# A two-block transformer kernel in f32: GpSimd's weight sums and tap matrices rescheduled, and the first products of three stages reordered

## The chip, the cores and the metric

The kernel runs on one core of one Trainium2 chip. The metric is the device time of one execution in microseconds (us). In the profile PE is TensorE, DVE is VectorE, ACT is ScalarE, POOL is GpSimd and SP is SyncE, which issues most DMAs.

## The reference, cut to what matters

The reference is a stack of residual layers in f32 over 512 positions of width 1024 (the later layers also carry 256 context positions). In order: latent attention, a squared-ReLU MLP, a gated mixer (`sgu`), a second MLP, a final norm, then a second network: convolution, an rwkv mixer, attention, convolution and the output norm. The parts that matter here are these.

```python
h = rms_norm(x, norm_mix[i]);  x = x + mixer(h)                      # x @ w_o ends each mixer
h = rms_norm(x, norm_ffn[i]);  x = x + square(relu(h @ w_up)) @ w_down
# gated mixer: z = gelu(h @ w_in); u, v = split(z); ...; (u * v) @ w_out
# convolution: a, b, gate = split(h @ w_in, 3); y = a * sigmoid(b)
#              y = depthwise_conv(y, 31 taps); y = silu(layernorm(y)); (y * silu(gate)) @ w_out
```

## The kernel before, in words

The activations lie transposed in SBUF: `xs` is the residual and `hn` the normed input, each 128 partitions by 8 rows of blocks (k = 0 to 7) by 768 positions.

**Products with fewer multiplications.** Twelve weight matrices (list `BLOCKED`) go through `pair_products`. One chunk of weights gives two output blocks from seven block products instead of eight (the Winograd form of Strassen's scheme). Each of the seven is a call of `product`: four matmuls of 128x256. It takes either a raw weight block (A0, A1, A3) or a sum of blocks (S1 to S4), and either a quarter of the input (b11, b21, b22) or a sum of quarters (t1 to t4). b11 and b12 are rows k = 0 to 3 of the input, b21 and b22 are rows 4 to 7; t1 = b12 - b11, t2 = b22 - t1, t3 = b22 - b12, t4 = t2 - b21. `mla_out` has 4 chunks, `up0` and `up1` 16 each, `sgu_u` 8, `sgu_out` and `attn_out` 4 pairs of 2 chunks, `down0` and `down1` 4 pairs of 4.

**Who makes the operands.** POOL makes the weight sums in `weight_sums` (lines 3321 to 3344): four additions of 128x512 for each chunk n, in the order of the chunks. For n >= 2 it waits until PE has finished chunk n - 2 (`chunk_mm` at n - 1), which frees the place of the sums. DVE makes t1 to t4 in `block_sums` (line 2611), counted by the semaphore `t_ready`. PE takes the seven products in a fixed order: A0, A1, S2, S3, S1, A3, S4. For the first chunk of a stage (`early`) three quarters of S4 come right behind A1, since S4 needs no sum of the input.

**Who empties the banks.** Products land in four quarter banks. ACT copies the first (`take_p1`), and DVE adds the parts in `take_first`, `take_second` and `take_third` (lines 2627 to 2654). PE may write a quarter again once `bank_ev` has reached its count.

**Stage borders.** `mla_out` and `sgu_out` end in `block_residual` (line 2678). For each of four pairs p it adds two rows into `xs` (line 2689) and writes the scaled rows of `hn` for the next MLP (line 2695), and each written row raises `h_ready` by one. Rows come as 2p + 1 and 2p, so that rows 0 to 3 are there after p = 1. The MLP's first product waits for all eight (`up_need`, line 1146). Behind `down0` comes a norm: ACT squares, POOL adds most squares, PE sums over partitions, ACT takes the root, DVE the reciprocal (line 2438) and eight SCALAR_TENSOR_TENSOR (line 2446) that give `hn`; then come `block_sums` and the stage `sgu_u`.

**Attention's last round.** The loop of units U has 8 rounds of 8 units i. In each unit DVE takes a maximum (line 3286), negates it (3288), waits for ACT's exponential, takes a reciprocal (3302) and scales the probabilities (3304). In the last round two block sums for `attn_out` stand in unit 5 and two in unit 6.

**The second convolution.** `conv` (name `c1`) starts with a norm of the residual. POOL adds six of the eight blocks of squares in `partial_sum` (line 3346), PE then adds that sum and the last two blocks over the partitions in `norm_sums`, and ACT and DVE finish the norm. The convolution of one of the eight rows of channels (k = 7) is done on PE, with 31 diagonal matrices that POOL builds in `tap_matrices` (line 3365): 31 TENSOR_SCALAR of 128x128. POOL's program ends with these lines:

```python
            weight_sums("attn_out")
            tap_matrices(1, chunk_mm, Q["attn_out"].chunk1)
            partial_sum("c1", SEQ, hn)
            partial_sum("last", SEQ, hn)
```

An engine runs its own program in order; a wait holds all that stands behind it.

Of the kernel before, what the change touches and what calls it, by code (L numbers as in the profile page):

```python
# [247 lines left out]
def build(nc, t):  # L248
# [18 lines left out]
    with ExitStack() as ctx:  # L267
# [647 lines left out]
        def _(pe):  # L915
# [190 lines left out]
            def pair_products(name, p, c, B, need):  # L1106

                b, B = Q[name], B[c]
                g, n = b.pair0 + p, b.chunk(p, c)
                end, first = bank_mm if c == b.per - 1 else None, c == 0  # L1110
                halves_need = name == "mla_out" and p == 0
                lo, hi = slice(0, HALF), slice(HALF, SEQ)

                def take(b_):
                    if first and g:
                        pe.wait_ge(bank_ev, bank_free(g - 1) + b_ + 1 if g - 1 != PAIR0 + WIDE_PAIRS - 1 else bank_free(g))

                pe.wait_ge(raw_full[raw_turn(n)], raw_count(n))
                take(0)
                need(c, 0)  # L1120
                product(name, p, c, quad_ps[0][:, lo], first, True, "A0", B["b11"])
                if halves_need:
                    need(c, -1)
                product(name, p, c, quad_ps[0][:, hi], first, False, "A1", B["b21"], end)
                early = p == 0 and c == 0
                if early:
                    take(3)
                    product(name, p, c, quad_ps[3][:, lo], first, True, "S4", B["b22"], ks=range(3))
                take(1)
                need(c, 2)  # L1130
                product(name, p, c, quad_ps[1][:, lo], first, True, "S2", B["t2"])
                need(c, 3)
                product(name, p, c, quad_ps[1][:, hi], first, False, "S3", B["t3"], end)
                take(2)
                product(name, p, c, quad_ps[2][:, lo], first, True, "S1", B["t1"])
                need(c, 4)
                product(name, p, c, quad_ps[2][:, hi], first, False, "A3", B["t4"], end)
                if not early:
                    take(3)
                product(name, p, c, quad_ps[3][:, lo], first, True, "S4", B["b22"], chunk_mm, ks=range(3, 4) if early else range(4))  # L1140

            def ffn(i, nrm):

                up, down = Q[f"up{i}"], Q[f"down{i}"]

                def up_need(c, t):
                    if t:
                        pe.wait_ge(t_ready, T_BASE[f"up{i}"] + t)
                    else:
                        pe.wait_ge(h_ready, 8 * (NI[nrm] + 1))  # L1150

                def down_need(c, t):
                    if t:
                        pe.wait_ge(t_ready, T_BASE[f"down{i}"] + 4 * c + t)
                    else:
                        pe.wait_ge(hid_ready, HID_BASE[i] + 8 * (c + 1))

                for p in range(up.pairs):
                    pair_products(f"up{i}", p, 0, up_b, up_need)
                    if p == 3:  # L1160
                        norm_sums(nrm, SEQ, seq_only(fsq[i]))
                    if p in UP_MOD_SUMS:
                        q = UP_MOD_SUMS.index(p)
                        mod_sums(MOD_UP[i] + q, up_macc[q % 2])
                for p in range(down.pairs):
                    for c in range(down.per):
                        pair_products(f"down{i}", p, c, down_b, down_need)
# [7 lines left out]

            def sgu_u_need(c, t):

                if t:
                    pe.wait_ge(t_ready, T_BASE["sgu_u"] + t)
                else:  # L1180
                    pe.wait_ge(h_ready, 8 * (NI["sgu"] + 1))

            def sgu_out_need(c, t):

# [1244 lines left out]
        def _(dve):  # L2429
# [178 lines left out]
                        o(stt(a, w, c, a, ALU.mult, ALU.add), (sig["half"] if k == 3 else sig["macc"] if k == KD - 1 else None) if v else None)  # L2608
                    last_step[v] = o.last

            def block_sums(B, ahead=True, rest=True):

                b11, b12, b21, b22, t1, t2, t3, t4 = [B[n] for n in ("b11", "b12", "b21", "b22", "t1", "t2", "t3", "t4")]
                T = sig["t"]
                if ahead:
                    o(nc.vector.tensor_tensor(t1, b12, b11, ALU.subtract), T)
                    o.wait()
                    o(nc.vector.tensor_tensor(t2, b22, t1, ALU.subtract), T)
                    T.two = T.n
                if rest:  # L2620
                    o(nc.vector.tensor_tensor(t3, b22, b12, ALU.subtract), T)
                    dve.wait_ge(T.sem, T.two)
                    o(nc.vector.tensor_tensor(t4, t2, b21, ALU.subtract), T)

            add = nc.vector.tensor_tensor

# [70 lines left out]
            block_sums(mla_b[0])  # L2697
            for p in range(Q["mla_out"].pairs):
                block_residual("mla_out", p, gain=0)

            def ffn(i, nrm):
                up, down = Q[f"up{i}"], Q[f"down{i}"]
                dve.wait_ge(h_ready, 8 * (NI[nrm] + 1))
                block_sums(up_b[0])
                for p in range(up.pairs):
                    g = up.pair0 + p
                    top, low = (hid[:, 2 * p, lo_t], hid[:, 2 * p, hi_t]), (hid[:, 2 * p + 1, lo_t], hid[:, 2 * p + 1, hi_t])
# [6 lines left out]
                dve.wait_ge(mod_mm, MOD_UP[i] + 6)  # L2714
                dve.wait_ge(hid_ready, HID_BASE[i] + 8)
                dve.wait_ge(chunk_mm, up.chunk1)
                block_sums(down_b[0], rest=False)
                take_third(up.chunk1, top, w_done)
                block_sums(down_b[0], ahead=False)
                for c in range(1, 4):  # L2720
                    dve.wait_ge(hid_ready, HID_BASE[i] + 8 * (c + 1))
                    block_sums(down_b[c])
# [15 lines left out]
            dve.wait_ge(mod_c, 1)  # L2738
            nc.vector.memset(small[:, 56:57], 0.0).then_inc(mod_mm, 1)
            ffn(0, "ffn0")  # L2740
            norm("sgu", SEQ, lambda k, c0: V("norm_mix", 8 + k), full_cols(hn), h_ready)
            dve.wait_ge(h_ready, 8 * (NI["sgu"] + 1))
            block_sums(sgu_u_b[0])
            for p in range(Q["sgu_u"].pairs):
                mod_beside(MOD_BESIDE["sgu_u"] + p // 2, range(4 * (p % 2), 4 * (p % 2) + 4))
                g = Q["sgu_u"].pair0 + p
# [51 lines left out]
            for p in range(Q["sgu_out"].pairs):  # L2798
                mod_beside(MOD_BESIDE["sgu_out"] + p, range(KD))
                block_residual("sgu_out", p, gain=1)  # L2800
            ffn(1, "ffn1")
            norm("first", SEQ, lambda k, c0: V("final_norm", k), full_cols(xs), h_ready)
            dve.wait_ge(mod_mm, MOD_CHUNKS + 1)
# [476 lines left out]
            for r in range(s.rounds):  # L3280
                for i in range(8):
# [10 lines left out]
                            head_out(2 * r - 2)  # L3292
                    if i == 4 and r:
                        head_out(2 * r - 1)
                    if i in (5, 6) and r == s.rounds - 1:
                        if i == 5:
                            dve.wait_ge(hd_ev, 8)
                        block_sums(attn_out_b[0], ahead=i == 5, rest=i == 6)
                    beside_unit(r + 1, i)
                    dve.wait_ge(sc_ev, U + 1)  # L3300
                    o.wait()
# [14 lines left out]
        def _(pool):  # L3316
# [4 lines left out]
            def weight_sums(name):  # L3321
# [5 lines left out]
                for n in range(b.chunk0, b.chunk1):  # L3327
# [5 lines left out]
                        pool.wait_ge(lin_mm, S["sgu_v"].tile1 if n == b.chunk0 else S["sgu_mix"].tile1)  # L3333
                    if name == "attn_out" and n == b.chunk0:
                        pool.wait_ge(qk_ready, 3 * 8)
                    if n >= 2:
                        pool.wait_ge(chunk_mm, n - 1)
                    pool.wait_ge(raw_full[raw_turn(n)], raw_count(n))
# [102 lines left out]
            for r in range(KD):  # L3441
                for n, x in enumerate([ak[r % 2][:, CTX:ALL], aq[r % 2][:, 0, :], aq[r % 2][:, 1, :]]):
                    pool.wait_ge(qk_norm, 3 * r + n + 1)
                    for p0 in range(0, P, 32):
                        p1 = p0 ^ 32
                        pool.dma_start(asw[p0:p0 + 32, n, :], x[p1:p1 + 32, :]).then_inc(swapped[n], 16)  # L3446
            weight_sums("attn_out")
            tap_matrices(1, chunk_mm, Q["attn_out"].chunk1)
            partial_sum("c1", SEQ, hn)
            partial_sum("last", SEQ, hn)  # L3450

    return nc
# [82 lines left out]
```

## Time and profile before

| what | value |
|---|---|
| time, median of 3 runs | 4170.13 us (4169.95 to 4173.42) |
| the profiled execution's own time | 4169.9 us |
| its span in the trace | 4168.1 us |
| PE busy | 3885.7 us, 93% |
| DVE busy | 2217.9 us, 53% |
| POOL busy | 989.5 us, 24% |
| ACT busy | 958.1 us, 23% |
| mean granted clock of PE | 0.98 of full |

The span is 1.8 us shorter than that execution's time. An f32 matmul shows up as two records in the timeline, so that a product of four matmuls is x8 and a chunk of seven products is x56. In the timeline a row gives start, duration, engine, line, operation, operands and count; the brackets hold the idle time of the engine before it and what ended that idle time.

### The profile page before, as it was taken

The numbers are of one execution on the slowest core, as the hardware profiler recorded it, in microseconds if no ns is written. First come the engines' busy times: TensorE is split into PE (matmuls) and PEld (weight loads), VectorE is DVE, ScalarE is ACT, GpSimd is POOL, SyncE is SP. The second block draws the span as 40 slices with busy tenths as digits, with TensorE's granted clock in tenths as the row PEclk, the third lists the DMA queues.
The fourth block names the chain that finished last, engine by engine and source line by source line (L and its number), as shares of the span: only waits on it lengthen the run. The fifth ranks groups of instructions, "written<-read, shape, count | busy, mean of one in ns | idle before, by whom it ended". The sixth has DMA issues, their size and how long they took to land. (4 is left out here: it accounts for less than half of the span.)

```text
span 4168.1 us, 75603 instructions
## 1 busy us (share of the span) xinstructions
PE 3885.7 (93%) x33270; PEld 2701.9 (65%) x33270; DVE 2217.9 (53%) x3439; ACT 958.1 (23%) x1759; POOL 989.5 (24%) x749
## 2 busy tenths in 40 slices
PE   7999999999999999999998888888899999989897
PEld 2478887758888855555555777777655555547343
DVE  2567814658685149936452455555315444452593
ACT  1411100110110020021014344433213344330102
POOL 0044544204445420002332224222001001014100
PEclk9999999999999999999999999999999999999999
DMA  1123323433342212112335211110112111112121
GB/s 65 44 102 142 111 90 104 170 131 122 131 142 86 77 51 60 41 41 76 106 96 182 72 35 34 48 43 33 60 36 71 38 56 59 38 38 71 51 71 41
DMA packets 148016, 319.20 MB, mean 77 GB/s; under 512 B 12720, under 2 KB 106928, under 8 KB 136816
## 3 DMA queue, kind: packets, MB, share of 16 engines
q1 hardware_dynamic: 143968, 303.96, 21.4%
q0 software_dynamic: 3728, 10.49, 1.0%
q8 instruction: 260, 4.26, 0.4%
q14 instruction: 60, 0.49, 0.0%
HBM read 276.67 MB, written 30.41 MB: 74 GB/s over the span
## 5 line engine op out<-in xcount | busy, mean ns | idle before, releaser
L917 PE MATMUL lin_ps<-hn,ring 128*128 128x256 f32 (+2 forms) x3968 | 1275.5, 477 | 33.9 <-DVE hn L2695 11.4
L917 PEld LDWEIGHTS lin_ps<-hn,ring 128*128 128x128 f32 (+1 forms) x3968 | 752.3, 191 | 508.4 <-issue 446.4
L917 PE MATMUL lin_ps<-arena 64*64 64x64 f32 (+5 forms) x9784 | 700.4, 258 | 82.7 <-ACT arena L1856 32.2
L917 PE MATMUL lin_ps<-arena,ring 128*128 128x256 f32 (+2 forms) x2800 | 711.1, 409 | 12.0 <-DVE arena L2893 7.6
L917 PEld LDWEIGHTS lin_ps<-arena 64*64 64x64 f32 (+2 forms) x9784 | 531.5, 144 | 179.8 <-issue 97.5
L917 PEld LDWEIGHTS lin_ps<-arena,ring 128*128 128x128 f32 (+1 forms) x2800 | 531.1, 191 | 162.8 <-issue 90.7
L1856 ACT ACTIVATE arena<-lin_ps 128x512 f32<-128x512 f32 (+3 forms) x495 | 250.7, 528 | 922.6 <-PE lin_ps L917 890.6
L2451 DVE SCALAR_TENSOR_TENSOR arena<-arena,vec 128x512 f32<-128x512 f32 (+3 forms) x499 | 392.6, 861 | 1.3
L2451 DVE SCALAR_TENSOR_TENSOR arena<-arena,cs 128x512 f32<-128x512 f32 x336 | 348.9, 1106 | 0.0
L917 PE MATMUL sum_ps<-arena 64*64 64x64 f32 (+1 forms) x7176 | 310.4, 224 | 22.1 <-issue 13.5
L917 PEld LDWEIGHTS sum_ps<-arena 64*64 64x64 f32 (+1 forms) x7176 | 262.0, 137 | 35.8 <-issue 21.4
L917 PE MATMUL out_ps<-arena 64*64 64x64 f32 (+2 forms) x2330 | 256.3, 284 | 7.3 <-issue 5.3
L1856 ACT ACTIVATE xs<-lin_ps 128x256 f32<-128x256 f32 x60 | 23.0, 383 | 840.3 <-PE lin_ps L917 840.3
L917 PEld LDWEIGHTS out_ps<-arena 64*64 64x64 f32 (+1 forms) x2330 | 153.0, 147 | 86.8 <-issue 79.9
L3286 DVE TENSOR_REDUCE small<-lin_ps 128x1 f32<-128x768 f32 x64 | 61.3, 958 | 257.7 <-PE lin_ps L917 257.1
L3339 POOL TENSOR_TENSOR ring<-ring 128x512 f32<-128x512 f32 x53 | 76.0, 1435 | 508.6 <-PE lin_ps L917 419.2
L3339 POOL TENSOR_TENSOR arena<-ring 128x512 f32<-128x512 f32 x53 | 75.9, 1432 | 477.4 <-PE lin_ps L917 371.0
L3446 POOL DMA_DIRECT2D arena<-arena x96 | 50.5, 533 | 566.9 <-DVE arena L2451 566.9
L3355 POOL TENSOR_TENSOR hn<-hn 128x512 f32<-128x512 f32 (+1 forms) x17 | 24.7, 1453 | 660.6 <-ACT hn L1856 660.0
L1856 ACT ACTIVATE arena<-sum_ps 128x128 f32<-128x128 f32 (+4 forms) x291 | 120.8, 415 | 255.0 <-PE sum_ps L917 200.6
L917 PE MATMUL lin_ps<-hn,arena 128*128 128x256 f32 x736 | 168.6, 379 | 0.0
L3058 DVE COPY_PREDICATED arena<-arena,lin_ps 128x512 f32<-128x512 int32 x96 | 70.0, 729 | 184.1 <-issue 184.0
(252 smaller groups left out, 4560.2 us busy)
## 6 DMA issues: line engine op xcount, KB each, us to landing
ring<-w_up SPq DMA_DIRECT2D x32, 1024.0 KB, 5.9
ring<-w_down SPq DMA_DIRECT2D x32, 1024.0 KB, 5.2
arena<-w_mod SPq DMA_DIRECT2D x24, 1024.0 KB, 7.8
arena<-w_mod SPq DMA_DIRECT2D x12, 2048.0 KB, 7.5
features<-arena SPq DMA_DIRECT2D x64, 384.0 KB, 6.2
ring<-w_attn SPq DMA_DIRECT2D x16, 1536.0 KB, 6.3
ring<-w_conv_in SPq DMA_DIRECT2D x16, 1024.0 KB, 5.8
ring<-features SPq DMA_DIRECT2D x40, 384.0 KB, 3.2
```

What stands on the lines that cost most here:

```text
L917: return pe.matmul(out, lhsT, rhs, start=start, stop=stop)
L1856: return nc.scalar.activation(out, in_, func, **kw)
L2451: return nc.vector.scalar_tensor_tensor(*a)
L3058: nc.vector.copy_predicated(by_step(F_[G % 2]), level_mask(l, 1), by_step(fz_ps)).then_inc(f_ready, 1)
L3286: o(nc.vector.tensor_reduce(small[:, 0:1], scs, AXX, ALU.max))
L3339: o(tt(s1, a21, a22, ALU.add), block)
L3355: o(nc.gpsimd.tensor_tensor(a, a, last_cols(dst[:, k, :], width), ALU.add), partial if k == last else None)
L3446: pool.dma_start(asw[p0:p0 + 32, n, :], x[p1:p1 + 32, :]).then_inc(swapped[n], 16)
```

## The change

- POOL's order at the end: `partial_sum("c1")` now stands ahead of `tap_matrices(1, ...)`.
- `weight_sums` gets one more wait at the second chunk of five stages. For `up0`, `up1` it waits for all eight rows of the scaled input, for `sgu_u` until the residual of `down0` is complete, for `sgu_out` until the four block sums of the first chunk are there, for `attn_out` until all head outputs are there.
- In `up0`, `up1` and `sgu_u` the first chunk's order becomes A0, S1, A1, three quarters of S4, S2, S3, A3, rest of S4 (name `lead`). A0 and S1 wait for four rows of the input and for t1 alone; A1 waits for all eight.
- `block_sums` takes a list of which sums to make. t1 of the MLPs is made behind the third pair of `block_residual`, t1 of `sgu_u` between the fifth and the sixth row of the norm. The four sums of `attn_out`'s first chunk stand in units 1, 2, 4 and 6 of the last round, one in each.

```diff
@@ pair_products
                 product(name, p, c, quad_ps[0][:, lo], first, True, "A0", B["b11"])
-                if halves_need:
+                early = p == 0 and c == 0
+                lead = early and name in ("up0", "up1", "sgu_u")
+                if lead:
+                    take(2)
+                    need(c, 1)
+                    product(name, p, c, quad_ps[2][:, lo], first, True, "S1", B["t1"])
+                if halves_need or lead:
                     need(c, -1)
                 product(name, p, c, quad_ps[0][:, hi], first, False, "A1", B["b21"], end)
-                early = p == 0 and c == 0
...
-                take(2)
-                product(name, p, c, quad_ps[2][:, lo], first, True, "S1", B["t1"])
+                if not lead:
+                    take(2)
+                    product(name, p, c, quad_ps[2][:, lo], first, True, "S1", B["t1"])
@@ up_need (sgu_u_need in the same way)
-                    if t:
+                    if t > 0:
                         pe.wait_ge(t_ready, T_BASE[f"up{i}"] + t)
                     else:
-                        pe.wait_ge(h_ready, 8 * (NI[nrm] + 1))
+                        pe.wait_ge(h_ready, 8 * NI[nrm] + (8 if t else 4))
@@ block_sums
-            def block_sums(B, ahead=True, rest=True):
+            def block_sums(B, which=(1, 2, 3, 4)):
...
+                for n in which:
+                    if n == 1:
+                        T.zero = T.n
+                        o(nc.vector.tensor_tensor(t1, b12, b11, ALU.subtract), T)
+                    if n == 2:
+                        dve.wait_ge(T.sem, T.zero + 1)
+                        o(nc.vector.tensor_tensor(t2, b22, t1, ALU.subtract), T)
+                    if n == 3:
+                        o(nc.vector.tensor_tensor(t3, b22, b12, ALU.subtract), T)
+                    if n == 4:
+                        dve.wait_ge(T.sem, T.zero + 2)
+                        o(nc.vector.tensor_tensor(t4, t2, b21, ALU.subtract), T)
@@ DVE's program
                 block_residual("mla_out", p, gain=0)
+                if p == 2:
+                    block_sums(up_b[0], (1,))
@@ ffn
                 dve.wait_ge(h_ready, 8 * (NI[nrm] + 1))
-                block_sums(up_b[0])
+                block_sums(up_b[0], (2, 3, 4))
@@
-            norm("sgu", SEQ, lambda k, c0: V("norm_mix", 8 + k), full_cols(hn), h_ready)
+            rd(SEQ, std_ready, NI["sgu"] + 1)
+            for k in range(KD):
+                if k == 5:
+                    dve.wait_ge(h_ready, 8 * NI["sgu"] + 4)
+                    block_sums(sgu_u_b[0], (1,))
+                stt(hn[:, k, CTX:ALL], xs[:, k, CTX:ALL], V("norm_mix", 8 + k), last_cols(rstd, SEQ), ALU.mult, ALU.mult).then_inc(h_ready, 1)
             dve.wait_ge(h_ready, 8 * (NI["sgu"] + 1))
-            block_sums(sgu_u_b[0])
+            block_sums(sgu_u_b[0], (2, 3, 4))
@@
                 block_residual("sgu_out", p, gain=1)
+                if p == 2:
+                    block_sums(up_b[0], (1,))
@@ attention, in the last round
-                    if i in (5, 6) and r == s.rounds - 1:
-                        if i == 5:
+                    if i in (1, 2, 4, 6) and r == s.rounds - 1:
+                        if i == 1:
                             dve.wait_ge(hd_ev, 8)
-                        block_sums(attn_out_b[0], ahead=i == 5, rest=i == 6)
+                        block_sums(attn_out_b[0], ([1, 2, 4, 6].index(i) + 1,))
@@ weight_sums
+                    if n == b.chunk0 + 1:
+                        if name == "up0" or name == "up1":
+                            pool.wait_ge(h_ready, 8 * (NI["ffn" + name[2]] + 1))
+                        if name == "sgu_u":
+                            pool.wait_ge(res_ready, RES_BASE["down0"] + 8)
+                        if name == "sgu_out":
+                            pool.wait_ge(t_ready, T_BASE["sgu_out"] + 4)
+                        if name == "attn_out":
+                            pool.wait_ge(hd_ev, HEADS)
                     if n >= 2:
                         pool.wait_ge(chunk_mm, n - 1)
@@ end of POOL's program
             weight_sums("attn_out")
+            partial_sum("c1", SEQ, hn)
             tap_matrices(1, chunk_mm, Q["attn_out"].chunk1)
-            partial_sum("c1", SEQ, hn)
             partial_sum("last", SEQ, hn)
```

## Rows read from the trace of the kernel before

**Rows 1.** The page: TensorE's busy time, its share of the span, and its instructions.

```profile
PE 3885.7 (93%) x33270; PEld 2701.9 (65%) x33270; DVE 2217.9 (53%) x3439; ACT 958.1 (23%) x1759; POOL 989.5 (24%) x749
```

**Rows 2.** Timeline of TensorE from the end of attn_out into the second convolution.

```profile
3834.07 12.25 PE L917 MATMUL lin_ps<-arena,ring 128*128 128x256 f32 x56
3872.15 4.87 PE L917 MATMUL sum_ps<-hn,con 128*128 128x512 f32 x6 [25.83 <-POOL hn L3355]
...
3882.81 7.53 PE L917 MATMUL lin_ps<-hn,ring 128*128 128x512 f32 x17 [1.50 <-ACT hn L1856]
```

**Rows 3.** Timelines of GpSimd (two rows) and ScalarE in the same stretch.

```profile
3846.42 18.73 POOL L3369 TENSOR_SCALAR arena<-con,vec 128x128 f32<-128x128 f32 x31 [18.22 <-PE lin_ps L917]
3865.12 6.88 POOL L3355 TENSOR_TENSOR hn<-hn 128x512 f32<-128x512 f32 x5
...
3847.67 1.41 ACT L1856 ACTIVATE hn<-xs 128x512 f32<-128x512 f32 x2 [9.56 <-DVE xs L2451]
```

**Rows 4.** DMA issues from 3840 to 3870 us: KB each, median us to landing.

```profile
ring<-w_conv_in SPq DMA_DIRECT2D x2, 1024.0 KB, 6.7
```

**Rows 5.** Timeline of VectorE: eight rows of a norm, beside tap_matrices(0) and then alone.

```profile
1482.78 6.19 DVE L2446 SCALAR_TENSOR_TENSOR xs<-xs,vec,rstd 128x512 f32<-128x512 f32 x8
...
695.35 5.39 DVE L2446 SCALAR_TENSOR_TENSOR hn<-xs,vec,rstd 128x512 f32<-128x512 f32 x8
```

**Rows 6.** Timeline of TensorE from the end of mla_out to up0's second chunk.

```profile
256.29 12.25 PE L917 MATMUL lin_ps<-arena,ring 128*128 128x256 f32 x56
275.06 5.46 PE L917 MATMUL lin_ps<-hn,ring 128*128 128x256 f32 x16 [6.52 <-DVE hn L2695]
...
288.99 8.80 PE L917 MATMUL lin_ps<-hn,ring 128*128 128x256 f32 x40
```

**Rows 7.** Busy times by slice, all engines (PEclk is the granted clock), up0's border.

```profile
272.00:274.00 2.00, 0.00 (x0) 0.00 (x0) 1.97 (x2) 0.46 (x1) 1.92 (x2) 0.50 1.11 411
```

**Rows 8.** Busy times of VectorE in residual rows, then PEclk, DMA share, GB/s.

```profile
269.11:274.91 5.80, 5.73 (x5) 0.73 0.84 299
1033.28:1035.61 2.33, 2.26 (x5) 1.00 0.93 387
681.98:688.39 6.41, 6.37 (x4) 0.72 0.88 312
1472.97:1475.74 2.77, 2.73 (x4) 1.00 0.00 0
```

**Rows 9.** Timeline of VectorE: one block sum alone and one beside GpSimd's sums.

```profile
274.95 1.22 DVE L2616 TENSOR_TENSOR hn<-hn 128x1024 f32<-128x1024 f32 x1
...
507.71 2.29 DVE L2616 TENSOR_TENSOR arena<-arena 128x1024 f32<-128x1024 f32 x1
```

**Rows 10.** Timeline of TensorE: the last work of sgu_out and the start of up1's second chunk.

```profile
1058.50 1.84 PE L917 MATMUL out_ps<-con,arena 128*128 128x1 f32 x16
...
1079.98 8.80 PE L917 MATMUL lin_ps<-hn,ring 128*128 128x256 f32 x40
```

**Rows 11.** Timeline of TensorE: the start of sgu_u's first and second chunk.

```profile
700.89 5.87 PE L917 MATMUL lin_ps<-hn,ring 128*128 128x256 f32 x16 [5.10 <-DVE hn L2446]
...
715.23 5.34 PE L917 MATMUL lin_ps<-hn,ring 128*128 128x256 f32 x24
```

**Rows 12.** Waits of TensorE from 3660 to 3760: total, times, longest.

```profile
PE sum_ps L1804 <- DVE std L3304: 6.2, 4, 3.0
PE sum_ps L1804 <- DVE rstd L3304: 4.3, 2, 2.4
```

**Rows 13.** Timeline of VectorE in attention's last round.

```profile
3717.45 0.16 DVE L3302 RECIPROCAL small<-small 128x1 f32<-128x1 f32 x1 [1.06 <-ACT rstd L1856]
...
3729.98 1.22 DVE L2618 TENSOR_TENSOR arena<-arena 128x1024 f32<-128x1024 f32 x1
```

**Rows 14.** Timelines at sgu_out's start: VectorE's last gated row, then TensorE's first products.

```profile
951.64 1.68 DVE L2794 TENSOR_TENSOR arena<-arena 128x512 f32<-128x512 f32 x1
...
954.04 17.49 PE L917 MATMUL lin_ps<-arena,ring 128*128 128x256 f32 x72 [2.61 <-DVE arena L2451]
```

More of the change, by code:

```diff
@@ L1176, in sgu_u_need @@
             def sgu_u_need(c, t):
-                if t:
+                if t > 0:
                     pe.wait_ge(t_ready, T_BASE["sgu_u"] + t)
                 else:
-                    pe.wait_ge(h_ready, 8 * (NI["sgu"] + 1))
+                    pe.wait_ge(h_ready, 8 * NI["sgu"] + (8 if t else 4))
             def sgu_out_need(c, t):
@@ L2609, in mod_step @@
                     last_step[v] = o.last
-            def block_sums(B, ahead=True, rest=True):
+            def block_sums(B, which=(1, 2, 3, 4)):
                 b11, b12, b21, b22, t1, t2, t3, t4 = [B[n] for n in ("b11", "b12", "b21", "b22", "t1", "t2", "t3", "t4")]
                 T = sig["t"]
[L2615 to L2623, printed above, removed]
+                for n in which:
[10 more added lines that the diff above has]
+                        o(nc.vector.tensor_tensor(t4, t2, b21, ALU.subtract), T)
             add = nc.vector.tensor_tensor
@@ L2716, in ffn @@
                 dve.wait_ge(chunk_mm, up.chunk1)
-                block_sums(down_b[0], rest=False)
+                block_sums(down_b[0], (1, 2))
                 take_third(up.chunk1, top, w_done)
-                block_sums(down_b[0], ahead=False)
+                block_sums(down_b[0], (3, 4))
                 for c in range(1, 4):
```

## The prediction

> **What bounds the kernel now.** The page comes first: TensorE is busy for 93% of the span [rows 1]. So time is to be won only where TensorE stands still or runs slowly, and an engine's relief counts by what TensorE waits less. The list of waits shows where these places are; the timeline around each shows what ended last. The change touches six.
>
> The largest is the border to the second convolution. TensorE stands for 25.83 us before the last products of the norm's sum [rows 2]. The releaser is GpSimd's fifth addition. GpSimd was not slow there: it sat idle for 18.22 us, then spent 18.73 us on the 31 tap matrices and only then 6.88 us on the partial sum [rows 3]. Nothing in that sum needs the end of `attn_out`: its squares come from pairs 0 to 2.
>
> The other places are stage borders at which DVE works out what the next stage reads, while GpSimd adds weights beside it. At `up0` TensorE stands for 6.52 us, and its first 16 records then take 5.46 us [rows 6], while 56 records take 12.25 in full stride, so 16 should take 3.5. The granted clock was 0.50, the 1.2 GHz level, inside that gap [rows 7]; before the gap TensorE had been busy. So a border costs its gap and a second part for the slow records behind it. Both go if the gap closes.
>
> **The change part by part.**
>
> *1. Partial sum ahead of the tap matrices.* GpSimd's idle 18.22 us take the 6.88 us. TensorE can then add block 0 at once, and what is late next is ACT's squares of the last pair: two in 1.41 us from 3847.67, done at 3849.08 [rows 3]. The last block is two records, and six took 4.87 us at a low clock, 0.81 each [rows 2]; at full clock half of that, 0.4, so the sum ends near 3850.0. Before, it ended at 3872.15 + 4.87 = 3877.02 [rows 2]. Gain 27.0 us. Behind it the chain to the first product (3882.81) is unchanged: 5.8 us. Its weights are no hindrance: their DMAs go out at the end of `attn_out`, 3846.4, and land 6.7 us later [rows 4], by 3853.1, and the product is then wanted at 3855.8. The tap matrices move nowhere; they end at 3865.2, and TensorE wants them only behind eight chunks of the convolution's input product. But they now run beside the norm. The reciprocal's contention has no row of its own price, and eight SCALAR_TENSOR_TENSOR took 6.19 us beside `tap_matrices(0)` against 5.39 alone [rows 5]: 0.1 each. TensorE takes the rows one by one, so 0.1 to 0.8 us is lost. I take none and keep 0.8 for the range.
>
> The Trainium skill speaks against this order. "SBUF — State Buffer", section "Who interferes with whom", says that a DVE instruction with two SBUF inputs and a GpSimd instruction that reads SBUF exclude each other, the later one blocking fully. By that rule part 1 would give about 23.5, since each row would stand behind one tap matrix.
>
> *2. Residual rows without GpSimd beside them (`up0`, `up1`, `sgu_u`).* The four residual instructions of `mla_out`'s last pair took 5.80 us beside weight sums, and the same four took 2.33 with GpSimd silent [rows 8]: 3.47 less. For `down0` 6.41 stand against 2.77 at the like place of `down1`, where GpSimd ran only tap matrices [rows 8]: 3.64 less.
>
> *3. Work for TensorE in that time.* A product is 8 records, 12.25 / 56 x 8 = 1.75 us [rows 6]. At `up0` A0 needs rows 0 to 3 (ready since pair 1), S1 needs t1, whose 1.22 us [rows 9] fall before the last pair where DVE waits for TensorE anyway. If that cover were gone it would delay a bank by 1.2 us. So TensorE works from 268.54 to 272.0, and all eight rows are there at 269.11 + 2.33 = 271.4. No gap is left. Late next are t2 to t4: GpSimd's held sums start at 271.4 and run beside them, at up to 2.29 us each [rows 9], so they end at 273.7, 276.0 and 278.3. TensorE wants them at 275.1, 276.8 and 278.5. It just fits; 0 to 0.5 us may be lost. The second chunk starts at 268.54 + 12.1 = 280.6 instead of 288.99 [rows 6]: 8.4 us.
> The same at `up1`: 1058.50 + 1.84 + 12.1 = 1072.4 instead of 1079.98 [rows 10]: 7.6 us. There t1 stands ahead of DVE's modulation steps of the last pair, behind which DVE waits for TensorE again; that hides it.
>
> *4. `sgu_u`.* The norm's eight instructions start at 695.35 - 3.64 = 691.7; each takes 5.39 / 8 = 0.67 us [rows 5, 8]. TensorE starts A0 at 694.4 (four rows) instead of 700.89. t1 is there at 696.3, so S1 ends at 698.0; the last three rows come at 698.4 and A1 starts. Stalls of 0.6 us in all: second chunk at 694.4 + 12.1 + 0.6 = 707.1 instead of 715.23 [rows 11]: 8.2 us. The gap ahead of A0 shrinks from 5.10 us to some 2.5. If the clock still falls in it, 700.89 to 715.23 against 12.1 shows the price, 2.2 us.
>
> *5. The held sums themselves.* The second chunk's sums now start at about 271.4, 1061.5 and 684.8. Five additions took 6.88 us [rows 3], so four take 5.5, at most 7 beside DVE. TensorE wants S2 of that chunk 3.5 us into it, at 284. Cost 0, with 6 us to spare. Queued behind them on GpSimd are only the third chunk's sums, which wait for the first chunk's end in any case.
>
> *6. `attn_out`.* In the last round TensorE waits 6.2 + 4.3 us for DVE's scaling [rows 12]. A unit leaves DVE 1.06 us idle under ACT's exponential [rows 13]. One block sum (1.22) fits nearly; the second lies fully in the chain, in two units. Spreading saves 2 x 1.2, and holding GpSimd's second chunk quickens one scaling (my estimate is 0.9, as GpSimd's sums nearly double a duration in rows 9); the sum in unit 1 runs beside the first chunk's (2.29 instead of 1.22) and unit 4, where a head output stands already, pays about 0.7. Net 2.5 us, between 0 and 5.
>
> *7. `sgu_out`.* The last gated row took 1.68 us beside the weight sums [rows 14]; half a lone block sum of twice its size is 0.6 [rows 9], so 1.0 goes. TensorE starts 1 us sooner, but at the end of the first pair it waits for DVE's modulation, and DVE has the same sums beside it, only later. I take 0.5, between 0 and 1.75 (x72 took 17.49 at 954.04 where 72 x 0.219 = 15.8).
>
> **Sum:** 27.0 + 8.4 + 7.6 + 8.2 + 2.5 + 0.5 = 54.2 us. The profiled execution took 4169.9 us, 0.2 under the median of the runs, so the two need no correction: 4169.9 - 54.2 = 4115.7 us.
>
> **The rivals.**
> - *DVE's slowness at the borders is not GpSimd's doing* (0.10). Then the rows come as late as before. `up0` stalls 3 us at A1, `up1` 1.4, `sgu_u` starts 3.6 later: 8 us less gain, 4124 us. Against it stand the two pairs of stretches [rows 8].
> - *The three stages give the border gain back inside* (0.08), because DVE's modulation or its DMA then ends last. Only parts 1 and 6 stay: 4140 us. For it: `sgu_u` shares DVE with modulation whose weights come by DMA. Against it: in the whole of these stages TensorE has no listed wait, and their loads are released by TensorE's own progress.
> - *The norm is slowed by the tap matrices* (0.05). If each of its eight rows waited for one of 0.60 us (18.73 / 31, [rows 3]), the last would come 4.8 us later, TensorE's first tile would end some 3.5 later: 4119 us. This is the rule of "SBUF — State Buffer" in the Trainium skill. Rows 5 speak against it.
> - *The reordered sum pays nothing* (0.02), if squares or weights turn out late by other work: 4143 us.
> - *Slower* (0.03). The place is S2 of every chunk in `up0`, `sgu_u`, `up1`: 40 chunks. If the hold left GpSimd behind for good, each chunk would wait. It decides from 54.2 / 40 = 1.4 us a chunk; at 2 us the time is 4169.9 - 54.2 + 80 = 4196 us. Against it: 5.5 to 7 us of sums in a period of 12.1, so any lag is gone after one chunk.
>
> **How the numbers follow.** The forecast has 0.72. Its own range is 4108 (attention 2.5 more, sgu_out 1.25 more, stalls of 1 us absent, some slow records fewer) to 4120 (attention 0, clock 2.2, small stalls). To reach 8 in 10 I take in the first and third rival and a margin for later stages that nothing here prices: 4106 to 4128. No change and 0.2% (8.3 us, about what a measurement of this kernel can tell) lie far off: faster 0.96, within 0.02, slower 0.02, the last two from the slower rival, a milder form of it, and what I may have overlooked.
>
> **What would show it.** TensorE's wait for GpSimd before the convolution's norm is gone from the list, and its first product follows `attn_out`'s end by 9 to 10 us. At `up0` and `up1` the gap is under 1 us and the clock stays 1.00; four residual instructions take 2.3 us. In `sgu_u` a gap of 2 to 3 us stays. The sums of the second chunks sit beside t2 to t4. I am wrong if TensorE shows new waits at A1, A3 or at the second chunk's S2, if the norm's rows take over 1 us beside the tap matrices, or if the stages between the borders grow longer.

## The result, and the profile after

| what | before | changed |
|---|---|---|
| median of 4 runs each | 4170.07 us (4169.95 to 4173.42) | 4132.44 us (4128.27 to 4136.49) |
| ratio | | 0.9908, 95% interval 0.9891 to 0.9925 |
| profiled execution's own time | 4169.9 us | 4131.3 us |

The kernel became 37.6 us faster. The forecast was 54.2 us faster, and its range ended at 4128: the direction was right, the size and the range were wrong.

The page of the changed kernel (TensorE's busy time answers to [rows 1]):

```profile
PE 3881.5 (94%) x33270; PEld 2702.8 (65%) x33270; DVE 2219.9 (54%) x3439; ACT 957.9 (23%) x1759; POOL 992.7 (24%) x749
```

Both kernels issue the same 33270 matmul records, in nearly the same order. So the start of the same record can be compared in both traces, which shows where time was won and lost. The table is worked out from the starts in the traces (changed kernel or experiment less the kernel before). A column is a place, given by its time in the trace of before; what changes between two columns happened in between. The experiments are told below; e11 has six records more than the others, which are left out.

```
at us:        24   254   295   666   719   950  1048  1087  1822  3019  3644  3845  3900  4150
changed      0.1  -2.9 -11.4 -11.4 -19.2 -19.4  -9.8 -17.4 -18.2 -10.1 -10.0 -12.9 -39.6 -38.2
e4 changed  -1.0  -3.9 -12.4 -12.4 -20.2 -20.4 -12.5 -20.1 -19.4  -4.5  -4.5  -7.5 -34.2 -34.3
e1          -0.1   2.7  -5.8  -5.8 -13.6 -13.9 -13.9 -21.5 -21.9 -18.2 -18.2 -21.0 -47.7 -46.3
e2          -0.3  -0.6   0.6   0.6   1.2   1.2   2.9   2.4   2.9   8.7   8.7   8.7 -18.0 -16.7
e3           0.0  -1.5  -1.6  -1.6  -1.6  -1.6   6.5   5.8   6.5  13.3  15.0  13.0  12.5  13.9
e5          -0.1  -4.0 -12.5 -12.5 -18.9 -18.9 -22.0 -29.6 -30.4 -38.7 -38.7 -42.1 -68.8 -70.3
e6           0.1   0.2  -2.2  -2.2  -6.8  -7.1  -7.1 -13.2 -14.0 -15.6 -15.6 -18.5 -45.2 -45.3
e7          -1.1  -0.8  -3.1  -3.1  -6.2  -6.1  -4.5  -8.9  -8.9  -9.6  -9.6 -11.6 -11.9 -12.0
e8           0.5   1.4  -7.1  -7.1 -15.5 -15.8 -15.8 -23.4 -23.7 -28.6 -26.9 -28.8 -55.5 -55.3
e9          -0.7  -3.6 -12.1 -12.1 -19.9 -20.1 -20.1 -27.8 -28.6 -30.0 -30.0 -30.4 -57.1 -55.8
e10         -0.4   2.0  -6.5  -6.5 -14.4 -14.6 -17.7 -25.4 -25.4 -29.8 -28.1 -31.5 -58.2 -59.7
e11         -0.2  -0.2  -8.7  -8.7 -17.8 -17.7 -20.8 -28.5 -29.3 -31.1 -31.1 -34.4 -61.1 -59.6
```

Row "changed": `up0`'s border (254 to 295) gave 8.5 us, `sgu_u`'s (666 to 719) 7.8, `up1`'s (1048 to 1087) 7.6, attention's last round (3644 to 3845) 2.9, the border to the second convolution (3845 to 3900) 26.7. Two stretches went the other way. `sgu_out` (950 to 1048) lost 9.6. The stretch from 1822 to 3019, which the change doesn't touch, lost 8.1.

Other stretches whose code is unchanged move too. From 24 to 254 us the rows move by between -3.9 (e5) and +2.8 us (e1), from 950 to 1048 e2 loses 1.7, and in attention's last round e3 and e7 gain 2.0. So one or two us in one row of the table are not told from this spread; where several rows show the same, they are.

**The second convolution's border.** TensorE's timeline in the changed kernel (against [rows 2]):

```profile
3820.82 12.25 PE L917 MATMUL lin_ps<-arena,ring 128*128 128x256 f32 x56
3832.91 1.02 PE L917 MATMUL sum_ps<-hn,con 128*128 128x512 f32 x2
3835.11 1.98 PE L917 MATMUL sum_ps<-hn,con 128*128 128x512 f32 x4 [1.18 <-ACT hn L1862]
...
3842.90 22.55 PE L917 MATMUL lin_ps<-hn,ring 128*128 128x512 f32 x52 [1.52 <-ACT hn L1862]
```

GpSimd's there (against [rows 3]), then VectorE's:

```profile
3814.91 6.90 POOL L3382 TENSOR_TENSOR hn<-hn 128x512 f32<-128x512 f32 x5
...
3833.18 20.51 POOL L3396 TENSOR_SCALAR arena<-con,vec 128x128 f32<-128x128 f32 x31 [11.37 <-PE lin_ps L917]
```

```profile
3837.86 3.35 DVE L2444 RECIPROCAL rstd<-std 128x512 f32<-128x512 f32 x1 [2.70 <-ACT std L1862]
3841.25 6.18 DVE L2452 SCALAR_TENSOR_TENSOR hn<-xs,modg,rstd 128x512 f32<-128x512 f32 x8
```

The wait of 25.83 us is gone; 1.18 us for ACT's squares is left. The partial sum sits in GpSimd's idle time. The tap matrices run beside the norm and stretch themselves (20.51 us for 18.73), while VectorE's eight steps take 6.18 us where 5.39 is the figure without them [rows 5].

**The border of `up0`.** TensorE, then VectorE in the changed kernel (against [rows 6, 8]):

```profile
253.07 12.25 PE L917 MATMUL lin_ps<-arena,ring 128*128 128x256 f32 x56
265.16 1.89 PE L917 MATMUL lin_ps<-hn,ring 128*128 128x256 f32 x8
266.88 1.89 PE L917 MATMUL lin_ps<-hn,arena 128*128 128x256 f32 x8
268.61 1.89 PE L917 MATMUL lin_ps<-hn,ring 128*128 128x256 f32 x8
...
277.24 8.80 PE L917 MATMUL lin_ps<-hn,ring 128*128 128x256 f32 x40
```

```profile
265.89 0.69 DVE L2698 TENSOR_TENSOR xs<-xs 128x512 f32<-128x512 f32 x1
266.62 0.49 DVE L2704 TENSOR_SCALAR hn<-xs,vec 128x512 f32<-128x512 f32 x1
...
269.40 2.29 DVE L2629 TENSOR_TENSOR hn<-hn 128x1024 f32<-128x1024 f32 x1
```

A0, S1 and A1 follow without a gap, and the second chunk starts 12.1 us after the first. GpSimd's held sums now run beside the block sums (2.29 us), which TensorE does not wait for. The granted clock stays full across the border (1.00; 0.50 in [rows 7]):

```profile
272.00:274.00 2.00, 2.00 (x11) 1.75 (x10) 2.00 (x2) 0.00 (x0) 2.00 (x2) 1.00 1.03 430
```

At `sgu_u` (against [rows 11]) the norm's sum takes 1.98 us instead of 3.78, a gap of 2.74 us stays ahead of A0, and the first eight records take 3.55 us instead of 1.75. The kernel before, then the changed kernel:

```profile
687.42 3.78 PE L917 MATMUL sum_ps<-hn,con 128*128 128x512 f32 x4 [5.08 <-ACT hn L1856]
```

```profile
672.97 1.98 PE L917 MATMUL sum_ps<-hn,con 128*128 128x512 f32 x4 [2.38 <-ACT hn L1862]
...
681.98 3.55 PE L917 MATMUL lin_ps<-hn,ring 128*128 128x256 f32 x8 [2.74 <-DVE hn L2457]
...
695.73 5.34 PE L917 MATMUL lin_ps<-hn,ring 128*128 128x256 f32 x24
```

**Where it lost: `sgu_out`.** TensorE in the changed kernel (against [rows 14]):

```profile
933.29 15.81 PE L917 MATMUL lin_ps<-arena,ring 128*128 128x256 f32 x72 [1.62 <-DVE arena L2457]
...
955.84 1.89 PE L917 MATMUL lin_ps<-arena 128*128 128x256 f32 x8
965.71 3.57 PE L917 MATMUL out_ps<-con,arena 128*128 128x1 f32 x16 [7.98 <-DVE arena L2457]
969.14 18.84 PE L917 MATMUL lin_ps<-arena,ring 128*128 128x256 f32 x72
```

The gap ahead of the stage is 1.0 us shorter, as forecast, and the first 72 records take 15.81 us instead of 17.49. Then TensorE stands for 7.98 us at the end of the first pair, before the 16 records that add VectorE's modulation product over the partitions. The kernel before: TensorE there and at the end of the third pair, then VectorE's fourteen steps for the first and the third pair:

```profile
980.52 1.95 PE L917 MATMUL out_ps<-con,arena 128*128 128x1 f32 x16 [0.35 <-DVE arena L2451]
...
1032.54 1.84 PE L917 MATMUL out_ps<-con,arena 128*128 128x1 f32 x16
```

```profile
967.06 13.41 DVE L2451 SCALAR_TENSOR_TENSOR arena<-arena,cs 128x512 f32<-128x512 f32 x14
...
1011.38 16.44 DVE L2451 SCALAR_TENSOR_TENSOR arena<-arena,cs 128x512 f32<-128x512 f32 x14
```

VectorE and GpSimd in the changed kernel:

```profile
946.43 2.89 DVE L2681 TENSOR_SCALAR arena<-arena,cs 128x512 f32<-128x512 f32 x2
949.25 16.41 DVE L2457 SCALAR_TENSOR_TENSOR arena<-arena,cs 128x512 f32<-128x512 f32 x14
```

```profile
938.88 2.13 POOL L3366 TENSOR_TENSOR arena<-ring 128x512 f32<-128x512 f32 x1 [27.31 <-DVE arena L2632]
...
947.59 1.45 POOL L3366 TENSOR_TENSOR ring<-ring 128x512 f32<-128x512 f32 x1
...
957.81 1.63 POOL L3366 TENSOR_TENSOR arena<-ring 128x512 f32<-128x512 f32 x1 [4.02 <-PE lin_ps L917]
```

The hold keeps GpSimd waiting until 938.88. Its sums for the second chunk then lie beside the block sums; those of the third, which before came 16.65 us after the second's, follow at once (947.59 to 953.80) and lie beside the modulation; and since this runs late, so do the fourth's (957.81 to 964.45). In the kernel before only one chunk's sums lay beside these fourteen steps (968.17 to 974.62); the next came at 980.25, after them. Two chunks instead of one: GpSimd adds for 4.55 + 6.64 = 11.2 us beside the fourteen steps and they take 16.41, against 6.45 us and 13.41. Alone they take 9.35 (e5). That is 7.06 / 11.2 = 0.63 and 4.06 / 6.45 = 0.63 us lost per us of GpSimd's additions, both times.

These 3.0 us are only a part of what the wait grew by, from 0.35 to 7.98. VectorE also begins the fourteen steps 2.9 us later after TensorE's first product of the stage (15.96 us, before 13.02): beside GpSimd three block sums took 2.17 to 2.29 us each instead of 1.22 (before, only two of the eight were so slow), and the two TENSOR_SCALAR 2.89 instead of 0.88. And TensorE, whose first 72 records were quicker, comes to the place 1.7 us sooner.

The first pair is the place that has no slack. In the third pair of the kernel before, the steps take 16.44 us beside 11.1 us of GpSimd's additions, and they cost nothing: TensorE comes to them at 1032.54, 4.7 us after they end.

The loss goes on behind the wait. The granted clock has fallen (1.00 became 0.50), and 16 + 72 records take 3.57 + 18.84 = 22.41 us instead of 1.95 + 15.79 = 17.74:

```profile
962.00:964.00 2.00, 0.00 (x0) 0.00 (x0) 2.00 (x2) 0.00 (x0) 1.92 (x2) 0.50 0.00 0
```

### The profile page after: what moved, and what is told of

Read it like the earlier page. It is cut to its first block and busy times, and to the rows that moved or that the text cites. A ratio compares the mean times of both kernels' runs of the same rounds, so it can differ in the third digit from the quotient of the medians.

```text
span 4129.5 us, 75607 instructions
## 1 busy us (share of the span) xinstructions
PE 3881.5 (94%) x33270; PEld 2702.8 (65%) x33270; DVE 2219.9 (54%) x3439; ACT 957.9 (23%) x1759; POOL 992.7 (24%) x749
```

## The experiments

Theory A: the hold of `sgu_out` costs, because it moves GpSimd's sums beside VectorE's modulation. Rivals: something else in the first pair is late, or the border terms were too large. Times of before were taken again with each group; they lay at 4176.98, 4169.88 and 4173.6 us on the chips used, so gains are taken within a group only.

**e1, e2, e3, e4 (one group; before 4176.98).**

e1 is the changed kernel without the hold of `sgu_out`:

```diff
-                        if name == "sgu_out":
-                            pool.wait_ge(t_ready, T_BASE["sgu_out"] + 4)
```

> The changed kernel without the wait of weight_sums at sgu_out's second chunk; all else as changed. Theory A (that wait pushes GpSimd's sums of chunks 2 and 3 under DVE's modulation, so that TensorE waits 8 us for it and then runs slowly): TensorE's wait for DVE before the modulation sums falls from 7.98 us to under 1, sgu_out from its first product to the end of its last modulation sum takes about 106 us instead of 116.9, and the time falls by 9 to 10 us, to about 4122. Rival B (DVE is late there because TensorE arrives earlier for other reasons; the wait itself costs nothing): the wait of 8 us stays and the time stays at 4130 to 4134.

Measured 4122.80 us (4118.94 to 4125.75), ratio 0.9866 (0.9849 to 0.9883), a gain of 54.2 us. TensorE, then VectorE:

```profile
966.75 1.95 PE L917 MATMUL out_ps<-con,arena 128*128 128x1 f32 x16 [0.34 <-DVE arena L2457]
```

```profile
953.29 13.40 DVE L2457 SCALAR_TENSOR_TENSOR arena<-arena,cs 128x512 f32<-128x512 f32 x14
```

The wait is back at 0.34 us and the steps at 13.40. From 950 to 1048 the table shows 0.0. Theory A holds. That the gain equals the forecast of 54.2 is chance; its interval runs from 49 to 63 us.

e2 is the kernel before with the second convolution's reordering alone:

```diff
-            tap_matrices(1, chunk_mm, Q["attn_out"].chunk1)
             partial_sum("c1", SEQ, hn)
+            tap_matrices(1, chunk_mm, Q["attn_out"].chunk1)
```

> The kernel before with partial_sum(c1) ahead of tap_matrices(1) and nothing else. My theory: 27 us, as in the trace of the changed kernel (the offset between the two traces moves by 26.6 us there), so 4143. If the 9 us that the changed kernel lost across the convolution and rwkv stages, whose code is the same, belong to the reorder (not likely, it comes later) they would show here; if they are the spread between executions, the traces of this kernel differ from before by as much, in either direction. Rival: by the rule of full exclusion between GpSimd and DVE the gain would be 23.5, 4146.6.

Measured 4150.27 us (4148.09 to 4153.18), ratio 0.9931 (0.9915 to 0.9948): 26.7 us gained, and 26.7 in the table. By the medians' interval it is 22 to 36 us, so it is the trace that excludes the rival's 23.5. VectorE:

```profile
3859.75 3.35 DVE L2438 RECIPROCAL rstd<-std 128x512 f32<-128x512 f32 x1 [2.69 <-ACT std L1856]
3863.14 6.18 DVE L2446 SCALAR_TENSOR_TENSOR hn<-xs,modg,rstd 128x512 f32<-128x512 f32 x8
```

e3 is the kernel before with the hold of `sgu_out` alone:

```diff
+                    if n == b.chunk0 + 1 and name == "sgu_out":
+                        pool.wait_ge(t_ready, T_BASE["sgu_out"] + 4)
```

> The kernel before with the one wait at sgu_out's second chunk (until its first chunk's four block sums). Theory A: the same loss as in the changed kernel, TensorE waits 7 to 8 us for DVE's modulation, and the time rises by 9 to 10 us to about 4180. Rival B: within 1.5 us of before. Rival C (the loss needs the earlier start of the changed kernel too): between 2 and 6 us.

Measured 4183.41 us (4179.56 to 4189.32), ratio 1.0017 (1.0008 to 1.0027): slower by 6.4 us. In the table it loses 8.1 us from 950 to 1048. TensorE:

```profile
983.77 3.57 PE L917 MATMUL out_ps<-con,arena 128*128 128x1 f32 x16 [7.99 <-DVE arena L2451]
```

So the hold alone costs: 3 to 11 us by the interval, which excludes rival B. Rival C's 2 to 6 us lies within the interval, but the wait is as long as in the changed kernel (7.99 and 7.98 us), so the loss does not need the changed kernel's earlier start.

e4 is the changed kernel again, on the chip of this group:

> The changed kernel once more, with a second profile. Open is the 9 us by which its TensorE fell back against the trace of before between 1480 and 3000 us, in stages that the change does not touch. If that is the spread between executions, this second trace differs from the first there by some us and its time lies between 4126 and 4137. If the change causes it, the same 9 us stand in the same place.

Measured 4134.21 us (4131.26 to 4135.55), ratio 0.9892 (0.9876 to 0.9909): 42.8 us gained, and 11.4 us behind e1. The hold of `sgu_out` is worth 11.4 us by the medians, 7.9 to 9.6 by the traces of the changed kernel. From 1822 to 3019 us the same kernel lost 14.9 us here and 8.1 in its first trace.

**e5, e6, e7, e8 (one group; before 4169.88).**

e5 holds the third chunk's sums as well, until the first pair's modulation is done:

```diff
+                    if n == b.chunk0 + 2 and name == "sgu_out":
+                        pool.wait_ge(mod_acc, MOD_BESIDE["sgu_out"] + 1)
```

> The changed kernel, hold at sgu_out's second chunk included, and its third chunk's weight sums held as well, until DVE has finished the first pair's modulation. Theory A (the loss comes from the sums of chunks 2 and 3 running beside DVE's 16 modulation instructions): those then take 10 to 12 us instead of 19.2, TensorE's wait at the modulation sums falls from 8 us to under 1.5, and the time is 8 to 10 us under the changed kernel's, within 2 us of the kernel without the hold. Rival B (a held second chunk makes the first pair late in itself): 7 us or more of wait stay, the time stays the changed kernel's or rises, since one more wait is added.

Measured 4106.55 us (4099.63 to 4116.35), ratio 0.9854 (0.9838 to 0.9871): 63.3 us gained. TensorE, VectorE and GpSimd:

```profile
934.33 15.81 PE L917 MATMUL lin_ps<-arena,ring 128*128 128x256 f32 x72 [1.62 <-DVE arena L2457]
```

```profile
949.27 9.35 DVE L2457 SCALAR_TENSOR_TENSOR arena<-arena,cs 128x512 f32<-128x512 f32 x14
```

```profile
958.70 1.27 POOL L3368 TENSOR_TENSOR ring<-ring 128x512 f32<-128x512 f32 x1 [10.03 <-DVE arena L2457]
```

With GpSimd silent the fourteen steps take 9.35 us, TensorE waits for them no more, and the stage gains 3.1 us instead of losing 9.6. The modulation still begins late (14.9 us after the first product, before 13.0), and that alone makes no wait. The hold was not wrong in itself: it ended too early for what came next on its engine.

e6 is e1 without the holds of `up0`, `up1` and `sgu_u`; the reordered products stay:

```diff
-                        if name == "up0" or name == "up1":
-                            pool.wait_ge(h_ready, 8 * (NI["ffn" + name[2]] + 1))
-                        if name == "sgu_u":
-                            pool.wait_ge(res_ready, RES_BASE["down0"] + 8)
```

> As e1_no_sgu_out_hold, and without the waits of weight_sums at up0, up1 and sgu_u too. If GpSimd's sums are what slows DVE at these borders: the four residual instructions take 5.8 us again instead of 2.3, TensorE stalls some 3 us at A1 in up0 and 1.4 in up1, sgu_u starts 3.6 us later; in all 8 us slower than e1, and 2 to 4 more if the clock falls again in one of the gaps. Rival (DVE's slowness has another cause): within 2 us of e1.

Measured 4122.45 us (4119.51 to 4130.72), ratio 0.9887 (0.9871 to 0.9904): 47.4 us gained. VectorE, then TensorE at `up0`:

```profile
271.98 1.75 DVE L2698 TENSOR_TENSOR xs<-xs 128x512 f32<-128x512 f32 x1
```

```profile
275.19 3.78 PE L917 MATMUL lin_ps<-hn,ring 128*128 128x256 f32 x8 [2.98 <-DVE hn L2704]
```

A residual step takes 1.75 us instead of 0.69, and TensorE stalls 2.98 us at A1: the first rival's picture and its 3 us, which come about only without the hold. The three borders give 2.4 + 4.6 + 6.1 = 13.1 us in the table, against 23.9 with the holds (e1 and the changed kernel alike). The 10.8 us between them fit the 8 to 12 that I expected; the medians show 6.8 us less than e1's gain, across two groups.

e7 is the kernel before with those three holds alone:

```diff
+                    if n == b.chunk0 + 1:
+                        if name == "up0" or name == "up1":
+                            pool.wait_ge(h_ready, 8 * (NI["ffn" + name[2]] + 1))
+                        if name == "sgu_u":
+                            pool.wait_ge(res_ready, RES_BASE["down0"] + 8)
```

> The kernel before with the waits at up0, up1 and sgu_u and nothing else. The holds alone bring the rows 3.5 us earlier at three borders, 10.6 us, plus what the shorter gap saves in slow records: 1.9 us at up0 and 2.7 at up1 if their gaps stay short enough for the clock not to fall. So 10.6 to 16 us under before. Rival: the reordered products carry the gain and the holds alone bring under 4.

Measured 4154.04 us (4150.08 to 4161.00), ratio 0.9962 (0.9948 to 0.9976): 15.8 us gained, while the table shows 2.3 + 3.1 + 4.4 = 9.8 at the borders. TensorE at `up0`:

```profile
271.17 6.61 PE L917 MATMUL lin_ps<-hn,ring 128*128 128x256 f32 x16 [3.05 <-DVE hn L2695]
```

The gap halves to 3.05 us, but the first 16 records still take 6.61 us instead of 3.5, so the trace stays under the 10.6 to 16 us expected, though above the rival's 4. The profiled execution was 4.2 us slower than the median, and 2.0 us of its gain lie in attention's last round, which this kernel leaves alone. Holds alone give 9.8 us and reordering alone 13.1; together they give 23.9.

e8 is e1 without the hold of `attn_out`:

```diff
-                        if name == "attn_out":
-                            pool.wait_ge(hd_ev, HEADS)
```

> As e1_no_sgu_out_hold, and without the wait at attn_out's second chunk; the four block sums stay spread. In the trace the attention's last round gained 2.8 us. If the hold carries a third of it (one scaling of 1.5 us back to 0.6), this kernel is about 1 us slower than e1, hard to tell by the time, but in its trace TensorE's gain across that round falls from 2.8 to about 2. Rival: the hold alone carries the gain and nothing of it is left.

Measured 4118.39 us (4114.04 to 4120.67), ratio 0.9877 (0.9860 to 0.9893). Attention's last round gains 1.9 us in the trace against 2.8 in e1. The 0.9 between them is less than the 2.0 by which kernels with the old code differ there (e2 0.0, e3 and e7 2.0), so that what the hold gives is not shown, by the trace or by the medians.

**e9, e10, e11 (one group; before 4173.6).**

e9 is e1 with `attn_out`'s block sums back in units 5 and 6:

```diff
-                    if i in (1, 2, 4, 6) and r == s.rounds - 1:
-                        if i == 1:
+                    if i in (5, 6) and r == s.rounds - 1:
+                        if i == 5:
...
-                        block_sums(attn_out_b[0], ([1, 2, 4, 6].index(i) + 1,))
+                        block_sums(attn_out_b[0], (1, 2) if i == 5 else (3, 4))
```

> As e1_no_sgu_out_hold, with the four block sums of attn_out back in units 5 and 6, the hold at its second chunk kept. In e8 (sums spread, no hold) TensorE gained 1.9 us across the last round in the trace, with both 2.8 to 3.4. So the spreading should carry about 2 and the hold about 1: here the gain across the round is about 1 us. Rival: the two overlap, and with the hold alone 2 us or more are left.

Measured 4117.15 us (4112.44 to 4125.48), ratio 0.9873 (0.9855 to 0.9890). The round gains 0.4 us in the trace, against 2.8 to 3.4 in the seven other traces that have both parts. So the spreading carries most of it, some 2.4 us by this one trace, with the same spread of 2.0 in mind; the medians cannot tell.

e10 is e5's kernel again, on another chip, for a second interval:

> The kernel of e5_hold_third_chunk_too once more, in five rounds: it was 63 us under before, 9 more than e1, whose difference in sgu_out is 8 us in the trace. If that holds, the ratio is between 0.984 and 0.988 and TensorE does not wait for the first modulation sums.

Measured 4111.43 us (4110.07 to 4113.53), ratio 0.9855 (0.9839 to 0.9872): 62.2 us gained. e5's gain repeats. Its interval lies clear of the changed kernel's in e4 (0.9876 to 0.9909), so this version beats both kernels. From e1 (0.9849 to 0.9883) the medians do not tell it apart; the trace does, with 3.1 us gained at `sgu_out` where e1 gains none.

e11 is e5's kernel with three more idle products, which keep TensorE busy, ahead of `sgu_u`:

```diff
             late_sums("sgu")
-            idle_products(5)
+            idle_products(8)
```

> The kernel of e5 with 8 instead of 5 idle products ahead of sgu_u, which fill the 2.7 us in which TensorE waits for the first four normed rows. In the changed kernel the first product behind that gap took 3.55 us instead of 1.9. Theory: 1.5 to 2 us less from the sum of the norm to sgu_u's second chunk in the trace, too little for the medians to tell. Rival: the idle products end too late and delay the first product, 0 to 1 us slower.

Measured 4113.13 us (4110.17 to 4115.27), ratio 0.9859 (0.9843 to 0.9876). TensorE at `sgu_u`, in e10 and then in e11:

```profile
687.18 3.47 PE L917 MATMUL lin_ps<-hn,ring 128*128 128x256 f32 x8 [2.74 <-DVE hn L2457]
```

```profile
677.81 7.03 PE L917 MATMUL out_ps<-con 128*128 128x512 f32 x16
685.01 1.96 PE L917 MATMUL lin_ps<-hn,ring 128*128 128x256 f32 x8 [0.17 <-DVE hn L2457]
...
697.44 5.36 PE L917 MATMUL lin_ps<-hn,ring 128*128 128x256 f32 x24
```

The gap of 2.74 us is filled and the eight records take 1.96 us instead of 3.47. A0 starts 9.02 us after the norm's last sum in both, and the second chunk follows A0 by 12.43 us, in e10 by 13.67 (its second chunk starts at 700.85). So the filling gives 1.2 us at this border, a little under the 1.5 to 2 expected, and the rival, that the idle products delay the first product, is out. In the whole time this does not show: e10 and e11 differ by less than their spread.

## Why the prediction was wrong in size

- **Part 1 was right.** 27.0 forecast, 26.7 measured in e2. Its small doubt too: the eight steps take 6.18 us beside the tap matrices, and the first product starts 9.8 us behind `attn_out`'s end, as foretold.
- **Parts 2 and 3 were right, part 4 in its size.** For `up0`, `up1` and `sgu_u` 8.4, 7.6 and 8.2 were forecast (715.23 - 707.1 is 8.1, not 8.2) and 8.5, 7.6 and 7.8 measured. At `sgu_u` luck helped: A0 started 7.5 us sooner than before where 6.5 were forecast, since the norm's sum became quicker too (1.98 us for 3.78), and the second chunk followed A0 by 13.75 us instead of 12.7, since the clock fell in the gap, which the forecast had named as a doubt and left out of its sum. e6 and e7 show that both halves are needed, and that VectorE's slowness at the borders is GpSimd's doing.
- **Part 6 came out, within a wide spread.** 2.5 forecast, 2.9 measured, while kernels with the old code gain 0.0 to 2.0 in the same round. e9 puts most of it down to the spreading; the hold's share is not shown. The forecast's own terms do not give 2.5 exactly: 2.4 + 0.9 - 0.7 is 2.6, and 1.5 if the longer sum of unit 1 counts in full.
- **Part 7 failed.** I took a gain of 0.5 us, between 0 and 1.75; `sgu_out` lost 9.6. I had written that at the end of the first pair TensorE waits for VectorE's modulation, and that it "has the same sums beside it, only later". They were not the same: the hold pressed the third chunk's sums against the second's, the block sums and the modulation ran late, and so the fourth's lay beside the modulation too. TensorE waited only 0.35 us there before, so that each us by which VectorE's chain ran late was a us of waiting, and the clock then fell. The lower bound of 0 left out a loss, though nothing excluded one. The trace of before could have warned of it: with two chunks' sums beside them the same fourteen steps take 16.44 us in the third pair against 13.41 in the first, where TensorE has 0.35 us of wait already, and a fallen clock behind a gap was priced at `up0`. The later start of the modulation would still have been missing from that sum.
- **Part 5 was right for its own question** and asked too little. The second chunk's S2 never waited. But part 5 looked at what was queued behind the hold, not at whom the moved sums would run beside. The slower rival went wrong in the same way: a hold can cost, but at VectorE's end in one place, not at S2 in 40 chunks.
- **The base.** With part 7 put right by +10.1 us the sum is 4125.8 us, inside the stated range. The changed kernel's median was 6.6 us above that, e4's gain of 42.8 us 1.3 below the 44.1 that this makes. The rest lies in stages that no part touches. From 1822 to 3019 us the kernels of this study, all with the same code there, stand between 8.3 us quicker (e5) and 14.9 slower (e4) than the profiled execution of before; e2 and e3 are 5.8 and 6.8 slower, e6 and e7 1.6 and 0.7 quicker. What sets this is open: no experiment isolated it. It is not the mean granted clock, which is 0.98 there in the kernel before, the changed kernel, e4 and e5. TensorE's idle time there that ends on nothing the profile shows is 52.1 us in e5 and 69.7 in e4, which is most of the 23.2 us between those two. The lead of e5's profiled execution is in part this spread (8.3 us). Of the 8 to 9 us by which the medians of e5 and e10 gain more than e1's, only 3.1 are shown in the stage that they change; the rest may be the same spread.
- **The rule of the Trainium skill** ("SBUF — State Buffer", section "Who interferes with whom") would have cut part 1 to 23.5 us. Here it is not borne out: 0.77 us a step beside 0.67 alone, not a whole tap matrix more. Where GpSimd has two inputs as well, its warning fits better: VectorE's residual step went from 0.69 to 1.75 us beside the weight sums (e6). Even there the fourteen steps lose 0.63 us per us of additions, not all of it.

## What to carry to other kernels

A wait that takes work out of one place puts it in another. List what the held engine will run back to back after release, and whom that meets; here the next chunk's sums had to be held too, and only then did the hold pay (e5). A chain for which the main engine already waits 0.35 us has no slack: price it as if it were critical. At a border, quicken the producer and give the consumer something to do: each alone brought 10 to 13 us, both together 24.

## What was not expected of the hardware

- Contention stretches both sides. GpSimd's addition took 2.13 us beside VectorE's block sums and 1.27 with VectorE idle (the line below, changed kernel); VectorE's fourteen steps took 9.35, 13.41 and 16.41 us with 0, 6.45 and 11.2 us of such additions beside them.

```profile
672.93 1.27 POOL L3366 TENSOR_TENSOR ring<-ring 128x512 f32<-128x512 f32 x1 [10.13 <-DVE xs L2747]
```

- Lateness feeds on itself: the slower modulation met a further chunk of sums that it had missed before, and the granted clock then halved within the wait, which cost 4.7 us on top of a wait of 7.98.
